# First chunk of the memory tokens loaded from ScalarE's queue, the last square in three pieces, and the low parts of a branch taken one step earlier

## The chip, the cores and the metric

The kernel runs on one core of one Trainium2 chip. The metric is the device time of one execution in microseconds; the kernel before takes 2140.35 us (median of 3 runs, 2139.76 to 2140.51).

## What is computed

One inference step of one encoder layer for two groups of tokens, 256 of a prompt and 64 of a sample, 320 in all, with width 2048:

```python
mkv = rmsnorm(mem_prompt, g_mem[l]) @ w_mem_kv[l]            # 256 memory tokens -> keys and values
xn = rmsnorm(x, g_mix)
(mq, mk, mv, mo, mi, mf, aq, ak, av, iq, ik, iw, cq, gt) = split_in(xn @ w_in)
# branch A: mLSTM; branch B: sparse attention over chosen keys; branch C: attention into the memory tokens
proj = jnp.einsum('btnc,ncd->btnd', branches, w_branch)
merged = jnp.sum(sigmoid(gates) * proj, axis=2)
h = x + merged @ w_out
y = h + (silu(gate) * val) @ w_down                           # [gate|val] = causal conv of rmsnorm(h) @ w_up
y_prompt, y_sample = rmsnorm(y, g_final)
```

All inputs, weights and outputs are float32.

## The kernel before, in words

**Number format.** Every large product is made from three products of float32r numbers: high part times high part, low times high, high times low. A weight arrives as float32 in units of 512 KB (128 rows of 8 blocks of 128 columns). ScalarE casts a unit to its high part (L956), VectorE subtracts to get its low part (L1360), TensorE then uses both (L548 to L550 for most of the kernel, L569 to L591 for the keys and values of the memory tokens). The units go through a ring of four slots: SyncE starts the load of a unit (`load`, L450) when VectorE is done with the slot's last use, and both `split` functions run two units ahead of TensorE (`LEAD`). Results collect in two PSUM banks in turn.

**Order of work.** Each engine has one program, written out by hand, and semaphores tie them together. (1) The memory tokens: 32 units, alternately for keys and values, while the tokens x are normalised. (2) The input projection, with the three branches woven in. (3) The merge: for each of 16 output tiles three gate tiles and three branch products (`merge_tiles`). (4) The output projection. (5) The feed-forward part in four groups, each with 11 pairs of up-projection tiles and then 16 tiles of the down-projection, which are added to `hT`. (6) The final norm.

**The start (L459 to L471, L650 to L671, L992 to L1003, L1458 to L1469).** The SyncE queue issues, one after the other, the first weight unit (L460), the gains of the norms (L461), the first four of the sixteen memory blocks in two transfers of two blocks (L463), three more weight units (L454) and the next four memory blocks (L432). Until the first product can be made TensorE multiplies zeros, `WARM` times (L652); VectorE writes these zeros (L1458) behind six semaphore increments. ScalarE loads a table for Sqrt (L993), casts half of the first unit (L997), waits for the gains and the first two memory blocks, scales these (L971), casts the other half and so on. VectorE makes the low part of the half unit (L1464), then the low parts of the memory blocks (L1388), in step with ScalarE.

**The merge (L1791 in VectorE's program).** In its first tile the last head pair of branch B is still being finished: ScalarE copies its high part out of PSUM (L1199, L1200), VectorE makes the low part (`q_los(3)`, L1764 and L1765). It does so in step m = 1 behind `split(pl, 9 * n + 6 + m)`, the low part of a weight unit. TensorE waits for it ahead of the product of branch B (L860), which is step m = 2.

**The end (L916 to L939, L1300 to L1341, L1942 to L1960).** The down-projection's last tile is added to `hT` by VectorE (L1832), ScalarE squares it (L1259, 320 columns at once) and scales it by the gain (L1303, L1304). The sum of squares over features is a product with a column of ones (`mm`, L598): three with the running sum `hacc`, three with the last square `h2`, each a pass over one group of tokens. Ahead of them TensorE turns the first output batch (`y_turns(0, 1)`, L928). VectorE and ScalarE then work out the inverse root (`rms`, L1374 to L1383), VectorE copies 64 of its values to other partitions for the sample (L1953), and both scale the ten turned batches, even ones on ScalarE (L1339), odd ones on VectorE (L1959). Five stores of 512 KB follow, each behind two batches (`y_store`, L410), four from SyncE's queue and one from ScalarE's.

Of the kernel before, what the change touches and what calls it, by code (L numbers as in the profile page):

```python
# [19 lines left out]
F32 = mybir.dt.float32  # L20
F32R = mybir.dt.float32r
ACT = mybir.ActivationFunctionType
# [65 lines left out]
MEM_SUM, MEM_ROW, X_SUM, X_ROW = 12, 14, 19, 21  # L88
WARM = 22
C_SLOTS = {2: (("scores", 0),), 3: (("probs", 0),), 4: (("values", 0), ("scores", 1)), 5: (("probs", 1),),  # L90
# [98 lines left out]
def layer(nc, a, o):  # L189

    with ExitStack() as ctx:
# [141 lines left out]
        hT = at("hT", R_BC, [KT, T])  # L333
        h2 = at("h_square", R_K + C_COS128 * 4, [T])
        hacc = at("h_square_sum", R_K + (C_COS128 + T) * 4, [3 * P])

# [21 lines left out]
        def sem(name):  # L358
            return ctx.enter_context(nc.semaphore(name))
# [4 lines left out]
        mem_in, x_in = [sem(f"mem_in{n}") for n in range(4)], [sem(f"x_in{n}") for n in range(4)]  # L364
        mem_first, hi_first, lo_first = (sem(n + "_first") for n in ("mem", "w_hi", "w_lo"))
        raw_in = [sem(f"raw_in{n}") for n in range(RING)]
# [33 lines left out]
            sem("f_" + n) for n in ("state", "ext", "tap2", "conv", "tanh", "y", "hi", "lo", "rms"))  # L400
        h_sq, h_sum, h_hi, h_lo, h_g = (sem("h_" + n) for n in ("square", "square_sum", "hi", "lo", "scaled"))
        y_T, y_act, y_dve, y_out, u_out = (
# [27 lines left out]
        def _(sp):  # L430
# [29 lines left out]
            sp.dma_start(raw[:, pl.slot(0), :, :].rearrange("p k c -> p (k c)"), a["w_mem"][0]).then_inc(raw_in[pl.slot(0)], 16)  # L460
            sp.dma_start(gcols[:, :, :].rearrange("p g k -> p (g k)"), a["gain_cols"]).then_inc(gains_in, 16)  # L461
            for n, done in enumerate((mem_first, mem_in[0])):
                sp.dma_start(memT[:, 2 * n:2 * n + 2, :].rearrange("p k t -> p (k t)"),  # L463
                             a["memT"][:, n * 2 * NMEM:(n + 1) * 2 * NMEM]).then_inc(done, 16)
            after = {3: (lambda: mem_chunk(1),), 5: (lambda: mem_chunk(2), identity), 7: (lambda: mem_chunk(3),),
# [63 lines left out]
        def _(pe):  # L529
# [388 lines left out]
            def y_turns(n0, n1):  # L918
                for n in range(n0, n1):
# [9 lines left out]
                    last.then_inc(y_T, 1)  # L929
            y_turns(0, 1)  # L930
            ones = K[:, C_ONE:C_ONE + 1]
            pe.wait_ge(h_sum, 2 * KT + 1)
            for u in range(3):
                mm(M[5][:, u:u + 1], hacc[:, u * P:u * P + P], ones, u == 0, False)
            pe.wait_ge(h_sq, 2 * KT)
            for u in (2, 0, 1):
                last = mm(M[5][0:X_ROWS[u], u:u + 1], h2[:, u * P:u * P + X_ROWS[u]], ones, False, u == 1)
            last.then_inc(sums, 1)
            y_turns(1, len(Y_BATCHES))  # L939

# [3 lines left out]
        @block.scalar  # L944
        def _(act):
            act.sem_inc(f_us, 1)
            act.sem_inc(bank_read[0], 1)
# [48 lines left out]
            for n in range(2):  # L996
                act.copy(whi[:, pl.slot(0), 4 * n:4 * n + 4, :], raw[:, pl.slot(0), 4 * n:4 * n + 4, :])\  # L997
                   .then_inc(w_hi if n else hi_first, 1)
                if n == 0:
                    act.wait_ge(gains_in, 16)  # L1000
                act.wait_ge(mem_in[0] if n else mem_first, 16)
                mem_his(n)
# [253 lines left out]
            def square(pl, e, k, summed):  # L1256
                act.wait_ge(bank_read[pl.bank(e)], pl.bank_read(e))
                act.wait_ge(h_sum, summed)
                act.activation(h2[:, :], hT[:, k, :], ACT.Square).then_inc(h_sq, 1)  # L1259
            for k0, k1, done in ((0, 2, hT_in), (2, KT, hT_rest)):  # L1260
# [38 lines left out]

            def h_tail(pl, e, k):  # L1300

                square(pl, e, k, k + (KT + 2))
                act.activation(hg[:, k, :], hT[:, k, 0:TP], ACT.Identity, scale=gcols[:, 3, ds(k, 1)])  # L1303
                act.activation(hgs[:, k, :], hT[:, k, TP:T], ACT.Identity, scale=gcols[:, 3, ds(k, 1)]).then_inc(h_g, 1)  # L1304
# [23 lines left out]
            for e in range(2):  # L1328
                h_tail(pl, e, KT - 2 + e)

# [16 lines left out]
        def _(dve):  # L1347
            own = Steps(dve, dve_own)
            dve.sem_inc(w_lo, RING)
            dve.sem_inc(c_lo, 2)  # L1350
# [106 lines left out]

            dve.memset(f32(zeros[:, :, :]), 0.0).then_inc(t_zero, 1)  # L1458
            dve.memset(warm[:, :], 1.0).then_inc(t_ones, 1)
# [331 lines left out]
            def merge_tiles(i, stages):  # L1791
                pl = place(U_G, T_G, i, 36, 24)
                for n in range(4):
# [5 lines left out]
                    for m, b in enumerate(BRANCHES):  # L1799
                        t = 6 * n + 3 + m  # L1800
                        split(pl, 9 * n + 6 + m)
                        if n == 0 and m == 1 and stages:
                            q_los(3)
                        dve.wait_ge(w_used, pl.through(9 * n + 6 + m))
                        if m == 0:
                            dve.wait_ge(m_lo, i * 4 + (n + 1))

                        bank = pl.bank(t)
                        dve.scalar_tensor_tensor(gtmp[:, :] if m else acc[:, :], th[:, b, :], 1.0, G[bank][:, 0:T],
                                                 ALU.add, ALU.mult).then_inc(bank_read[bank], 1)  # L1810
                        dve.wait_ge(bank_read[bank], pl.bank_read(t))
                        if m:
                            add = dve.tensor_tensor(acc[:, :], acc[:, :], gtmp[:, :], ALU.add)
                            if m == 1:
                                own.did(add)
                                own.settle()
                            else:
                                add.then_inc(m_sum, 1)
# [15 lines left out]
            def add_square(squared, summed):  # L1834
                dve.wait_ge(h_sq, squared)
                dve.wait_ge(h_sum, summed)
                dve.tensor_tensor(hacc[:, 0:T], hacc[:, 0:T], h2[:, :], ALU.add).then_inc(h_sum, 1)

# [70 lines left out]
            for g in range(GROUPS):  # L1909
# [5 lines left out]
                if g < GROUPS - 1:  # L1915
# [5 lines left out]
                    with dve.Fori(1, KT // 2) as i:  # L1921
                        pl = place(u0, t0, i, 4, 2)
                        for e in range(2):
                            split(pl, 2 * e, 2 * e + 1)
                            add_h(pl, e, i * 2 + e)
            dve.wait_ge(variances, 3)
            dve.memset(hacc[:, :], 0.0).then_inc(h_sum, 1)
            pl = place(u0, t0)
# [15 lines left out]
            add_square(2 * KT - 2, 2 * KT - 1)  # L1944
            for e in range(2):
                add_h(pl, e, KT - 2 + e)
                if e == 0:
                    add_square(2 * KT - 1, 2 * KT)
            dve.wait_ge(sums, 2)
            rms(3, 3, M[5][:, 0:3], fnv)  # L1950
            dve.wait_ge(dve_own, own.n)
            dve.sem_inc(f_rms, 2)
            dve.tensor_copy(fnv[TS:P, 2, 2:3], fnv[0:TS, 2, 2:3]).then_inc(f_rms, 1)  # L1953
            for n in range(1, len(Y_BATCHES), 2):
                u, q = Y_BATCHES[n]
                dve.wait_ge(y_T, n + 1)
                if u == 2:
                    dve.wait_ge(f_rms, 3)
                dve.tensor_scalar(ytok[:, u, q * 4 * P:(q + 1) * 4 * P], y_banks[n % 7][:, :],  # L1959
                                  fnv[:, 2, u:u + 1], None, ALU.mult).then_inc(y_dve, 1)  # L1960


# [235 lines left out]
```

## Time and profile before

| | |
|---|---|
| median of three runs | 2140.35 us (2139.76 to 2140.51) |
| profiled execution, its own time | 2139.86 us |
| its span, first to last instruction | 2138.0 us |
| TensorE busy (matmuls) | 2128.4 us, 100% of the span |
| VectorE / ScalarE / GpSimd busy | 1222.2 / 904.8 / 105.1 us |
| DMA | 329.40 MB, mean 154 GB/s |
| granted TensorE clock | 0.999 |

The span is 1.86 us shorter than the execution's own time; that part lies outside the instructions. Busy times of different engines overlap, so they don't add up to the span. A timeline row gives the start and the duration of an instruction (or of a run of equal ones) in us, the engine, the line, what is written and read, and in brackets how long the engine had been idle and what ended that.

### The profile page before, as it was taken

The numbers are of one execution on the slowest core, as the hardware profiler recorded it, in microseconds if no ns is written. First come the engines' busy times: TensorE is split into PE (matmuls) and PEld (weight loads), VectorE is DVE, ScalarE is ACT, GpSimd is POOL, SyncE is SP. The second block draws the span as 40 slices with busy tenths as digits, with TensorE's granted clock in tenths as the row PEclk, the third lists the DMA queues.
The fourth block names the chain that finished last, engine by engine and source line by source line (L and its number), as shares of the span: only waits on it lengthen the run. The fifth ranks groups of instructions, "written<-read, shape, count | busy, mean of one in ns | idle before, by whom it ended". The sixth has DMA issues, their size and how long they took to land.

```text
span 2138.0 us, 39690 instructions
## 1 busy us (share of the span) xinstructions
PE 2128.4 (100%) x14445; PEld 2107.6 (99%) x14445; DVE 1222.2 (57%) x1933; ACT 904.8 (42%) x1519; POOL 105.1 (5%) x160
## 2 busy tenths in 40 slices
PE   9999999999999999999999999999999999999998
PEld 8899999999999999999999999999999999999998
DVE  7846645545644444443445666656665666656675
ACT  6534433334433333333333444434444444444455
POOL 2203301103200000000000000000000000000000
PEclk9999999999999999999999999999999999999999
DMA  8644444443344444444454444454444444454443
GB/s 314 225 163 134 159 147 149 143 153 124 108 149 148 153 143 151 155 142 154 148 197 156 139 157 142 141 163 143 155 135 158 153 146 139 149 164 148 146 139 130
DMA packets 96607, 329.40 MB, mean 154 GB/s; under 512 B 11640, under 2 KB 19960, under 8 KB 96384
## 3 DMA queue, kind: packets, MB, share of 16 engines
q1 hardware_dynamic: 92624, 315.44, 44.6%
q0 software_dynamic: 3456, 9.49, 1.5%
q10 hardware_dynamic: 432, 3.15, 0.4%
q8 instruction: 67, 1.10, 0.2%
q14 instruction: 28, 0.23, 0.0%
HBM read 321.30 MB, written 6.73 MB: 153 GB/s over the span
## 4 chain that ended last, share of the span: by engine, by line
PE 99%; DVE 0%; DMA 0%; ACT 0%; issue 0%; SPq 0%; DVEq 0%; ACTq 0%
PE bank L550 30%; PE bank L549 30%; PE bank L548 30%; PE bank L598 3%; PE bank L569 1%; PE bank L595 1%; PE bank L586 1%; PE bank L587 1%; PE bank L591 1%; PE bank L906 1%; PE bank L907 1%; PE bank L905 1%; PE bank L571 1%; DMA memT<-in_memT 0%; PE bank L574 0%; PE bank L576 0%
## 5 line engine op out<-in xcount | busy, mean ns | idle before, releaser
L548 PE MATMUL bank<-xn_hi,w_hi 128*128 128x320 f32 (+1 forms) x3088 | 957.5, 310 | 0.0
L550 PE MATMUL bank<-xn_hi,w_lo 128*128 128x320 f32 (+1 forms) x3088 | 952.5, 308 | 0.0
L549 PE MATMUL bank<-xn_lo,w_hi 128*128 128x320 f32 (+1 forms) x3088 | 952.4, 308 | 0.0
L1360 DVE TENSOR_TENSOR w_lo<-w_raw,w_hi 128x1024 fp32r<-128x1024 f32 x625 | 744.8, 1228 | 329.2 <-ACT w_hi L956 327.5
L956 ACT CAST w_hi<-w_raw 128x1024 fp32r<-128x1024 f32 x625 | 631.2, 1047 | 184.8 <-PE bank L550 148.1
L548 PEld LDWEIGHTS bank<-xn_hi,w_hi 128*128 128x128 f32 x3088 | 580.0, 188 | 2.5 <-issue 1.9
L549 PEld LDWEIGHTS bank<-xn_lo,w_hi 128*128 128x128 f32 x3088 | 580.1, 188 | 0.5
L550 PEld LDWEIGHTS bank<-xn_hi,w_lo 128*128 128x128 f32 x3088 | 579.9, 188 | 0.0
L550 PE MATMUL bank<-y_hi,w_lo 128*128 128x320 f32 x616 | 189.9, 308 | 0.0
L548 PE MATMUL bank<-y_hi,w_hi 128*128 128x320 f32 x616 | 189.9, 308 | 0.0
L549 PE MATMUL bank<-y_lo,w_hi 128*128 128x320 f32 x616 | 189.9, 308 | 0.0
L1276 ACT ACTIVATE conv<-u_ext,conv_cols 128x322 f32<-128x322 f32 x88 | 58.0, 659 | 249.5 <-DVE u_ext L1869 249.5
L548 PE MATMUL bank<-branch_hi,w_hi 128*128 128x320 f32 x384 | 118.9, 310 | 0.4 <-DVE branch_lo L1765 0.4
L549 PE MATMUL bank<-branch_lo,w_hi 128*128 128x320 f32 x384 | 118.7, 309 | 0.0
L550 PE MATMUL bank<-branch_hi,w_lo 128*128 128x320 f32 x384 | 118.7, 309 | 0.0
L548 PEld LDWEIGHTS bank<-y_hi,w_hi 128*128 128x128 f32 x616 | 115.6, 188 | 0.0
L549 PEld LDWEIGHTS bank<-y_lo,w_hi 128*128 128x128 f32 x616 | 115.6, 188 | 0.0
L550 PEld LDWEIGHTS bank<-y_hi,w_lo 128*128 128x128 f32 x616 | 115.6, 188 | 0.0
L1832 DVE TENSOR_TENSOR hT<-hT,bank 128x320 f32 (+1 forms) x80 | 39.0, 487 | 131.6 <-PE bank L550 131.5
L963 ACT ACTIVATE gate_tanh<-bank 128x320 f32<-128x320 f32 x48 | 21.0, 438 | 201.8 <-PE bank L550 201.8
L1873 DVE SCALAR_TENSOR_TENSOR conv<-u_ext,conv_cols,conv 128x322 f32<-128x322 f32 x88 | 48.8, 555 | 91.3 <-ACT conv L1276 91.3
L1868 DVE TENSOR_TENSOR u_ext<-bank,ffn_norm_var 128x256 f32<-128x256 f32 x88 | 37.4, 425 | 84.7 <-PE bank L550 83.2
(339 smaller groups left out, 1963.6 us busy)
## 6 DMA issues: line engine op xcount, KB each, us to landing
w_raw<-in_w_in SPq DMA_DIRECT2D x210, 512.0 KB, 3.5
w_raw<-in_w_up SPq DMA_DIRECT2D x176, 512.0 KB, 3.9
w_raw<-in_w_down SPq DMA_DIRECT2D x64, 512.0 KB, 3.5
w_raw<-in_w_branch SPq DMA_DIRECT2D x48, 512.0 KB, 3.3
w_raw<-in_w_mem SPq DMA_DIRECT2D x32, 512.0 KB, 5.3
w_raw<-in_w_out SPq DMA_DIRECT2D x32, 512.0 KB, 4.0
w_raw<-in_w_down SPq DMA_DIRECT2D x64, 192.0 KB, 3.1
xT<-in_xT SPq DMA_DIRECT2D x4, 640.0 KB, 8.7
```

The lines of the kernel that those rows point to most:

```text
L548: pe.matmul(out, h, hi[:, k0 + k, c0:n], start=un == 0 and k == 0, stop=False)
L549: pe.matmul(out, h, lo[:, k0 + k, c0:n], start=False, stop=False)
L550: last = pe.matmul(out, l, hi[:, k0 + k, c0:n], start=False, stop=un == len(units) - 1 and k == nk - 1)
L569: pe.matmul(out[:, :].rearrange("p (s m) -> p s m", s=2), h[:, k, c], mboth[:, :, k_, :], start=k_ == 0, stop=False)
L571: last = pe.matmul(out[:, 0:NMEM], l[:, k, c], mhi[:, k_, :], start=False, stop=k_ == KT - 1)
L598: return pe.matmul(out, lhsT, rhs, start=first, stop=last)
L956: act.copy(whi[:, pl.slot(j), :, :], raw[:, pl.slot(j), :, :]).then_inc(w_hi, 1)
L1276: act.activation(cbuf[:, e, 0:T + 2], ext[:, e, 2:E2], ACT.Identity, scale=ccols[:, 2, ds(col, 1)], bias=ccols[:, 3, ds(col, 1)]).then_inc ...
L1360: dve.tensor_tensor(wlo[:, pl.slot(j), :, :], raw[:, pl.slot(j), :, :], f32(whi[:, pl.slot(j), :, :]), ALU.subtract).then_inc(w_lo, 1)
L1832: dve.tensor_tensor(hT[:, k, :], hT[:, k, :], G[b][:, 0:T], ALU.add).then_inc(bank_read[b], 1)
L1868: dve.tensor_tensor(ext[:, e, 2:2 + TP], G[b][:, 0:TP], fnv[:, 2, 0:TP], ALU.mult)
L1873: own.did(dve.scalar_tensor_tensor(c, ext[:, e, 1:T + 3], ccols[:, 1, ds(col, 1)], c, ALU.mult, ALU.add))
```

## The change

The first four memory blocks are loaded by one transfer of 512 KB from ScalarE's queue, as ScalarE's first instruction, and the gains by a second behind it; both leave SyncE's queue, and the semaphore `mem_first` goes. TensorE's multiplications of zeros become 24, and VectorE writes the zeros ahead of its semaphore increments. In the merge `q_los(3)` is placed ahead of the split of m = 1. The last tile is added and squared in three pieces (128, 128 and 64 columns), and TensorE takes each piece as it comes; `h2` grows from 320 to 384 columns, the last 64 of which are set to zero long before. The first output batch is turned behind the sums. The copy of the 64 values comes behind VectorE's first output batch.

```diff
-WARM = 22
+WARM = 24
...
-        h2 = at("h_square", R_K + C_COS128 * 4, [T])
-        hacc = at("h_square_sum", R_K + (C_COS128 + T) * 4, [3 * P])
+        h2_all = at("h_square", R_K + C_COS128 * 4, [3 * P])
+        h2 = h2_all[:, 0:T]
+        hacc = at("h_square_sum", R_K + (C_COS128 + 3 * P) * 4, [3 * P])
...
# SyncE
             sp.dma_start(raw[:, pl.slot(0), :, :].rearrange("p k c -> p (k c)"), a["w_mem"][0]).then_inc(raw_in[pl.slot(0)], 16)
-            sp.dma_start(gcols[:, :, :].rearrange("p g k -> p (g k)"), a["gain_cols"]).then_inc(gains_in, 16)
-            for n, done in enumerate((mem_first, mem_in[0])):
-                sp.dma_start(memT[:, 2 * n:2 * n + 2, :].rearrange("p k t -> p (k t)"),
-                             a["memT"][:, n * 2 * NMEM:(n + 1) * 2 * NMEM]).then_inc(done, 16)
...
# TensorE
-            y_turns(0, 1)
             ones = K[:, C_ONE:C_ONE + 1]
             pe.wait_ge(h_sum, 2 * KT + 1)
             for u in range(3):
                 mm(M[5][:, u:u + 1], hacc[:, u * P:u * P + P], ones, u == 0, False)
-            pe.wait_ge(h_sq, 2 * KT)
-            for u in (2, 0, 1):
-                last = mm(M[5][0:X_ROWS[u], u:u + 1], h2[:, u * P:u * P + X_ROWS[u]], ones, False, u == 1)
+            for u in range(3):
+                pe.wait_ge(h_sq, 2 * KT + u)
+                last = mm(M[5][:, u:u + 1], h2_all[:, u * P:u * P + P], ones, False, u == 2)
             last.then_inc(sums, 1)
-            y_turns(1, len(Y_BATCHES))
+            y_turns(0, len(Y_BATCHES))
...
# ScalarE
+            act.dma_start(memT[:, 0:4, :].rearrange("p k t -> p (k t)"), a["memT"][:, 0:4 * NMEM]).then_inc(mem_in[0], 16)
+            act.dma_start(gcols[:, :, :].rearrange("p g k -> p (g k)"), a["gain_cols"]).then_inc(gains_in, 16)
...
                 if n == 0:
                     act.wait_ge(gains_in, 16)
-                act.wait_ge(mem_in[0] if n else mem_first, 16)
+                    act.wait_ge(mem_in[0], 16)
                 mem_his(n)
...
+            def last_square():
+                act.wait_ge(h_sum, 2 * KT + 1)
+                for u in range(3):
+                    act.wait_ge(h_last, u + 1)
+                    t = slice(u * P, u * P + X_ROWS[u])
+                    act.activation(h2[:, t], hT[:, KT - 1, t], ACT.Square).then_inc(h_sq, 1)
...
# VectorE
             own = Steps(dve, dve_own)
+            dve.memset(zeros[:, :, :].bitcast(F32), 0.0).then_inc(t_zero, 1)
             dve.sem_inc(w_lo, RING)
...
-                        split(pl, 9 * n + 6 + m)
                         if n == 0 and m == 1 and stages:
                             q_los(3)
+                        split(pl, 9 * n + 6 + m)
...
+            dve.memset(h2_all[:, T:3 * P], 0.0)
             dve.memset(hacc[:, :], 0.0).then_inc(h_sum, 1)
...
-            for e in range(2):
-                add_h(pl, e, KT - 2 + e)
-                if e == 0:
-                    add_square(2 * KT - 1, 2 * KT)
+            add_h(pl, 0, KT - 2)
+            add_square(2 * KT - 1, 2 * KT)
+            dve.wait_ge(w_used, pl.through(3))
+            b = pl.bank(1)
+            for u in range(3):
+                t = slice(u * P, u * P + X_ROWS[u])
+                dve.tensor_tensor(hT[:, KT - 1, t], hT[:, KT - 1, t], G[b][:, t], ALU.add).then_inc(h_last, 1)
+            dve.wait_ge(h_last, 3)
+            dve.sem_inc(bank_read[b], 1)
...
             dve.sem_inc(f_rms, 2)
-            dve.tensor_copy(fnv[TS:P, 2, 2:3], fnv[0:TS, 2, 2:3]).then_inc(f_rms, 1)
             for n in range(1, len(Y_BATCHES), 2):
...
+                if n == 1:
+                    dve.tensor_copy(fnv[TS:P, 2, 2:3], fnv[0:TS, 2, 2:3]).then_inc(f_rms, 1)
```

## Rows read from the trace of the kernel before

**Rows 1.** The page, part 1: busy us of each engine, share of the span.
```profile
PE 2128.4 (100%) x14445; PEld 2107.6 (99%) x14445; DVE 1222.2 (57%) x1933; ACT 904.8 (42%) x1519; POOL 105.1 (5%) x160
```

**Rows 2.** All waits of TensorE's matmuls: waiter, releaser, us in total, times, longest.
```profile
PE bank L652 <- DVE zeros L1458: 2.1, 1, 2.1
PE bank L548 <- DVE branch_lo L1765: 0.4, 1, 0.4
PE bank L569 <- DVE mem_hi_lo L1388: 0.3, 1, 0.3
```

**Rows 3.** Timeline of the first 9 us: start, duration, engine, line, operation.
```profile
0.99 0.40 SPq L460 DMA_DIRECT2D w_raw<-in_w_mem  x1
1.21 1.28 ACT L993 ACT_TABLE_LOAD   x1 [1.21 <-PEq L2188]
...
1.70 0.38 DVE L1458 MEMSET zeros<- 128x384 f32 x1 [1.70 <-PEq L2188]
1.92 0.90 SPq L463 DMA_DIRECT2D memT<-in_memT  x2
...
2.13 5.06 PE L652 MATMUL bank<-zeros 128*128 128x256 f32 x22 [2.13 <-DVE zeros L1458]
...
4.34 0.62 ACT L997 CAST w_hi<-w_raw 128x512 fp32r<-128x512 f32 x1 [1.64 <-DMA w_raw<-in_w_mem]
4.99 0.69 DVE L1464 TENSOR_TENSOR w_lo<-w_raw,w_hi 128x512 fp32r<-128x512 f32 x1 [2.90 <-ACT w_hi L997]
6.20 0.91 ACT L971 ACTIVATE mem_hi_lo<-memT,norm_gains 128x256 fp32r<-128x256 f32 x2 [1.24 <-DMA memT<-in_memT]
...
7.46 0.76 PE L569 MATMUL bank<-mem_hi_lo,w_hi 128*128 128x512 f32 x1 [0.27 <-DVE mem_hi_lo L1388]
...
8.02 0.35 PE L571 MATMUL bank<-mem_hi_lo,w_lo 128*128 128x256 f32 x1
```

**Rows 4.** DMA issues near 2.4 us: count, KB each, median us to landing.
```profile
memT<-in_memT SPq DMA_DIRECT2D x2, 256.0 KB, 4.3
```

**Rows 5.** Timeline of the merge's first tile, ScalarE, VectorE and TensorE.
```profile
600.56 0.27 ACT L1200 CAST branch_hi<-bank 128x128 fp32r<-128x128 f32 x1
...
601.88 1.23 DVE L1360 TENSOR_TENSOR w_lo<-w_raw,w_hi 128x1024 fp32r<-128x1024 f32 x1 [3.29 <-ACT w_hi L956]
603.02 0.68 DVE L1764 TENSOR_TENSOR branch_lo<-bank,branch_hi 128x512 fp32r<-128x512 f32 x1
603.62 0.28 DVE L1765 TENSOR_TENSOR branch_lo<-bank,branch_hi 128x128 fp32r<-128x128 f32 x1
...
603.25 0.31 PE L550 MATMUL bank<-branch_hi,w_lo 128*128 128x320 f32 x1
604.22 0.32 PE L549 MATMUL bank<-branch_lo,w_hi 128*128 128x320 f32 x1
```

**Rows 6.** Timeline of the end, from the last tile's last product on.
```profile
2125.42 0.49 DVE L1832 TENSOR_TENSOR hT<-hT,bank 128x320 f32<-128x320 f32 x1 [3.33 <-PE bank L550]
...
2125.95 0.47 ACT L1259 ACTIVATE h_square<-hT 128x320 f32<-128x320 f32 x1 [3.73 <-DVE hT L1832]
...
2126.47 0.81 PE L598 MATMUL bank<-shape_consts,h_square 128*64 128x1 f32 x6
2126.72 0.33 ACT L1304 ACTIVATE h_scaled_sample<-hT,norm_gains 128x64 f32<-128x64 f32 x1
...
2127.32 0.16 DVE L1374 TENSOR_SCALAR ffn_norm_var<-bank 128x3 f32<-128x3 f32 x1 [1.40 <-PE bank L598]
...
2128.65 0.15 DVE L1953 COPY ffn_norm_var<-ffn_norm_var 64x1 f32<-64x1 f32 x1
2128.83 3.38 DVE L1959 TENSOR_SCALAR y_tokens<-bank,ffn_norm_var 128x512 f32<-128x512 f32 x5
...
2129.66 1.00 SPq L416 DMA_DIRECT2D out_y_prompt<-y_tokens  x2
```

**Rows 7.** DMA between 2129 and 2138 us, in 40 slices: GB/s.
```profile
GB/s 0 0 0 0 0 0 164 400 419 382 382 419 419 419 382 364 437 400 346 437 419 437 400 346 419 419 401 419 382 419 401 400 437 364 437 182 0 0 0 0
```

More of the change, by code:

```diff
@@ L364, in layer @@
         mem_in, x_in = [sem(f"mem_in{n}") for n in range(4)], [sem(f"x_in{n}") for n in range(4)]
-        mem_first, hi_first, lo_first = (sem(n + "_first") for n in ("mem", "w_hi", "w_lo"))
+        hi_first, lo_first = (sem(n + "_first") for n in ("w_hi", "w_lo"))
         raw_in = [sem(f"raw_in{n}") for n in range(RING)]
@@ L400, in layer @@
             sem("f_" + n) for n in ("state", "ext", "tap2", "conv", "tanh", "y", "hi", "lo", "rms"))
-        h_sq, h_sum, h_hi, h_lo, h_g = (sem("h_" + n) for n in ("square", "square_sum", "hi", "lo", "scaled"))
+        h_sq, h_sum, h_hi, h_lo, h_g, h_last = (sem("h_" + n) for n in ("square", "square_sum", "hi", "lo", "scaled", "last_tile"))
         y_T, y_act, y_dve, y_out, u_out = (
@@ L1258, in square @@
                 act.wait_ge(h_sum, summed)
-                act.activation(h2[:, :], hT[:, k, :], ACT.Square).then_inc(h_sq, 1)
+                act.activation(h2, hT[:, k, :], ACT.Square).then_inc(h_sq, 1)
+            def last_square():
[4 more added lines that the diff above has]
+                    act.activation(h2[:, t], hT[:, KT - 1, t], ACT.Square).then_inc(h_sq, 1)
             for k0, k1, done in ((0, 2, hT_in), (2, KT, hT_rest)):
@@ L1298, in up, with h_tail @@
                 conv_inputs(pl, 1, pair, pair + FT)
-            def h_tail(pl, e, k):
-                square(pl, e, k, k + (KT + 2))
+            def h_tail(pl, e, k, last=False):
+                if last:
+                    last_square()
+                else:
+                    square(pl, e, k, k + (KT + 2))
                 act.activation(hg[:, k, :], hT[:, k, 0:TP], ACT.Identity, scale=gcols[:, 3, ds(k, 1)])
@@ L1328, in _ @@
             for e in range(2):
-                h_tail(pl, e, KT - 2 + e)
+                h_tail(pl, e, KT - 2 + e, e == 1)
             root(4, 3, fnv)
@@ L1456, in x_lo @@
                 lo_part(xlo[:, 2 * q:2 * q + 2, :], xsc[:, q % 2, :, :], xhi[:, 2 * q:2 * q + 2, :], n_lo)
-            dve.memset(f32(zeros[:, :, :]), 0.0).then_inc(t_zero, 1)
             dve.memset(warm[:, :], 1.0).then_inc(t_ones, 1)
@@ L1836, in add_square @@
                 dve.wait_ge(h_sum, summed)
-                dve.tensor_tensor(hacc[:, 0:T], hacc[:, 0:T], h2[:, :], ALU.add).then_inc(h_sum, 1)
+                dve.tensor_tensor(hacc[:, 0:T], hacc[:, 0:T], h2, ALU.add).then_inc(h_sum, 1)
             dve.memset(hacc[:, :], 0.0).then_inc(h_sum, 1)
```

## The prediction, made before the changed kernel was run

> **What bounds the kernel now.** First I read the page's busy times: TensorE's matmuls fill 2128.4 of 2138.0 us, VectorE and ScalarE about half of it [rows 1]. So a gain can only come from where TensorE has nothing to do, or from outside its work. Next, the waits of TensorE's matmuls: there are three in the whole execution, 2.1 us for the zeros at the start, 0.3 us for the first memory block, 0.4 us for branch B's low part [rows 2]. That leaves the two ends, which I read in the timeline: from 0 to 7.46 us, before the first real product starts [rows 3], and from 2125.4 us, where the last product of the down-projection is through, to 2138 [rows 6]. In between there is nothing to win but the 0.4 us. The three places of the change are these three, and together they hold some 20 us, most of it transfers and short chains that stay. The change is therefore worth one or two us of 2140, whichever way it goes.
>
> **The merge.** VectorE does the low part of a weight unit at 601.88 (1.23 us) and only then branch B's low part, 603.02 to 603.90. But the high part that it needs was out of ScalarE at 600.56 + 0.27 = 600.83, and VectorE was idle for 3.29 us before 601.88, waiting for the unit's high part [rows 5]. In the new order it takes branch B's part from 600.85 to 601.75 (0.68 and 0.28 us, which overlap a little), and the unit's split still starts at 601.88. So the two operations are hidden by idle time, with 0.1 us to spare; if that cover went, the split would come later by as much, and the product of m = 1, which ran without a wait, does not need that unit (the splits run two units ahead). TensorE started its last product of m = 1 at 603.25 and the second product of branch B at 604.22. At the mean spacing of 2128.4 / 14445 = 0.147 us [rows 1] it would have been 603.54. Gain 0.68 us; the bounds are 0.4, the wait itself [rows 2], and 0.7.
>
> **The end, the last square.** Before: add 2125.42 to 2125.91, square 2125.95 to 2126.42, six passes with the last square 2126.47 to 2127.28, VectorE's first step of the root at 2127.32 [rows 6]. After, the adds of 128, 128 and 64 columns start one behind the other. A piece of 128 columns from PSUM took VectorE 0.28 us [rows 5], and operations in a row overlap by some 0.08, so the adds end near 2125.70, 2125.90 and 2126.05. ScalarE's squares follow each by 0.04; 64 columns take it 0.33 us [rows 6], so the last ends at about 2126.42, as before: the split saves nothing on these two engines. It saves on TensorE, where four of the six passes are over by then. Two are left, a third of 0.81, with their drain about 0.35 us instead of 0.81. Gain 0.46. Bounds: if three adds cost 0.49 each and the square 0.47, the last square ends at 2127.40 and the step is late by 0.47; if the pieces cost no more than the whole (adds 0.49 in all, last square 0.33), it is early by 0.60. I take 0.45.
>
> **The end, the order of turning and copying.** The first output batch is now turned behind the sums. A batch is four fp32 transposes, at 0.135 us a pass (0.81 for six) some 0.5 us, so the two batches that ScalarE and VectorE need first are there 1.1 us after the sums, while the chain of the root takes from 2127.32 to 2128.65, 1.33 us [rows 6]. That hides it; if transposes take 0.1 us more each than I read, the start of the outputs is late by the excess. The copy of the 64 values moves behind VectorE's first batch: that starts at 2128.65 in place of 2128.83, gain 0.18 (bounds 0, if ScalarE's half of the store decides, and 0.18).
>
> What is this worth at the end of the kernel? The stores are the last thing. From 2130.4 to 2137.0 the transfers run at about 400 GB/s without a hole [rows 7]: five stores of 0.52 MB need 6.6 us. VectorE makes a batch in 3.38 / 5 = 0.68 us [rows 6], and so a store is ready every 0.68 us, against 1.3 us that the engines take for it. The end is thus bound by the transfers, and it moves with the first store, not with the last batch. The first store was issued at 2129.66, behind VectorE's first batch; it comes earlier by 0.45 + 0.18 = 0.63 us, and so does the end. Bounds -0.5 and 0.78.
>
> **The start.** Two paths lead to the first product. From the memory blocks: the first two, with their wait counted by ScalarE, were there at about 6.12, ScalarE went on at 6.20, the product started at 7.46, 1.34 us after landing. From the first weight unit: landed at about 4.3, cast 4.34, low part 4.99 to 5.68 [rows 3]. In the new kernel VectorE needs from that landing 0.04 + 0.62 + 0.03 + 0.69 and then the memory block's low part, 0.5 with its hand-over: 1.9 to 1.95 us. Today this path has slack; it won't have any.
> SyncE's queue loses three issues (gains and two of the memory), so weight units 1 to 3 go out about 1.5 us earlier. ScalarE gains two issues ahead of its table load, some 0.45 us each by SyncE's rows, so that the load moves from 1.21 to about 2.1 and ends at 3.4, still ahead of 4.3: hidden. The memory chunk goes out at 1.0 in place of 1.92, but it is 0.52 MB in one piece, and it moves beside the weight unit, not behind it. The rows show no two queues at once at the start, so the price is bounded. Best: both land before TensorE is through with the zeros. The zeros are written first, at about 1.15 instead of 1.70, and TensorE starts at 1.55; 24 products at 5.06 / 22 = 0.23 us take it to 7.05 [rows 3]. Gain at most 0.45. Worst: both land only when the same bytes had landed before, with the second memory transfer at about 2.4 + 4.3 = 6.7 [rows 4]; then the first product is at 6.7 + 1.95 = 8.65, a loss of 1.2. Between them: the weight unit alone had landed at 4.3, and another 0.52 MB at the 400 GB/s of rows 7 add 1.3: both at 5.6, the small gains transfer just behind, the product at 5.6 + 1.95 = 7.55. That is where it was.
> To this comes the clock. The warm-up products have a spacing of 0.23 us for 256 columns, the lower level (1.2 GHz), and the first real one 0.56 us for 512 columns, from 7.46 to 8.02; the next ones run at the upper level. It rose 5.9 us after TensorE began. If it rises as long after the earlier start, at 7.45, the first product loses half of its 0.56. I take +0.2 for the clock and -0.1 for the landing: gain 0.1 us, range -1.2 to +0.75. Behind the first product nothing waits: TensorE has no other wait in the first 26 us [rows 2], and all loads come earlier.
>
> The Trainium skill bears on this: "DMA: Bandwidth & Descriptors", section "Issuing engines are not separate DMA queues", says that transfers started by different engines end up on the same 16 DMA engines and interleave, and that starting them from several engines saves only the issue time. It speaks against this part: by it the memory's lead of 0.9 us is paid for by the first weight unit. No row here shows two queues side by side at the start. Taken at its word, it makes the start worth between nothing and a loss, which is the first rival.
>
> **The sum.** 0.1 + 0.68 + 0.63 = 1.4 us. Profiled execution 2139.86 - 1.4 = 2138.45; the 1.86 us outside the span stay. The median shown, 2140.35, stands 0.49 above the profiled one, so the prediction is 2138.9 us. The other edits (64 columns set to zero by VectorE before the last group's down-projection, three more semaphore steps, a changed address) lie under TensorE's work.
>
> **Rivals.**
> (a) The shared transfer engines: both land at 6.7, the start loses 1.2 and the rest gains 1.31. About 2140.2. For it: the slow landing of rows 4. Against: those were transfers with half-size rows behind the gains.
> (b) The start gains all it can, 0.45 and 0.3 of clock, in all 2.06: 2138.3. For it: the smaller count of issues; against: the weight path's 1.95 us.
> (c) The pieces cost more than they save, -0.47 + 0.18 + 0.68 + 0.1: 0.5 in all, 2139.85. Against: the 0.28 us of rows 5.
> (d) Slower than before: the table load comes first on ScalarE and holds its queue. It ends at 1.21 + 1.28 = 2.49; the memory then needs 4.3 [rows 4] and 0.6 for its other half, the first product is at 7.4 + 1.34 = 8.75. TensorE is idle 1.7 us behind its zeros. The idle time of 0.27 us before did not bring the clock down; if this does, 5.9 us of real work run at the lower level and lose half of that. -1.3 - 2.9 + 1.31 = -2.9: 2143.2. It decides from a first product at about 8.8 without any loss of clock, and earlier with one. For it: the load stands at 1.21, as early as anything on ScalarE. Against: the two issues stand ahead of it in the program.
>
> **Chances.** Forecast (a sum of 0.9 to 1.9 us) 0.60, (a) 0.17, (b) 0.13, (c) 0.04, (d) 0.06. The shown runs lie within 0.75 us, so 0.4 us come on either side. The range 2137.8 to 2140.6 holds the forecast, (b), (c) and most of (a). A measurement can tell a difference of 0.2%, 4.3 us, from no change; none of the cases is that large, (d) included, so "the same" has 0.95, faster 0.02, slower 0.03 for what I have not seen.
>
> **What would show it.** In the changed kernel's waits branch B's low part is gone and its split still starts at about 601.9 less the start's shift. At the end, VectorE's first step of the root comes 1.5 us (before: 1.9) after the first add, and the first store 3.6 us after it (before: 4.24), with a gapless 6.6 us of transfer behind. At the start the first real product is at 7.5; at 7.1 (b) is right, at 8.5 or later (a) or (d), told apart by where the table load stands. The forecast is wrong if a new wait of TensorE appears in the first 30 us, or if the last store no longer ends with the transfers.

## The result and the profile after

The changed kernel takes 2142.43 us (median of 22 runs, 2140.91 to 2143.79); the kernel before, run as often beside it, 2139.86 (2139.13 to 2140.51). The ratio is 1.0013, 95% interval 1.0007 to 1.0019: slower by 2.6 us, where 1.4 us faster was forecast. That is under the 0.2% that the prediction thought could be told from no change, but with 22 runs of each the interval is narrower than that; it is outside the range, and it has a form: 3 of the 22 executions took 2140.9 to 2141.0 us, 13 took 2142.3 to 2142.6, 6 took 2143.4 to 2143.8. The profiled one is of the lowest group (2140.93, span 2139.0), so its trace shows a loss of 1.0 us and not what the median lost on top. In the measurements below, five single executions, of the kernel before too, took 3230 to 9571 us; the ratios leave such slow ones out, and no median shown would move by more than 0.05 us without them.

The waits of TensorE's matmuls in the changed kernel, which answer to [rows 2]:

```profile
PE bank L566 <- DVE mem_hi_lo L1397: 2.2, 1, 2.2
PE bank L649 <- DVE zeros L1357: 1.6, 1, 1.6
PE bank L595 <- ACT h_square L1264: 0.2, 1, 0.2
```

Branch B's wait is gone and the zeros come 0.5 us earlier, but the wait ahead of the first real product has grown from 0.3 to 2.2 us. The timeline of the start, to be read beside [rows 3]:

```profile
0.99 0.42 ACTq L942 DMA_DIRECT2D memT<-in_memT  x1
0.99 0.40 SPq L461 DMA_DIRECT2D w_raw<-in_w_mem  x1
...
1.43 0.46 ACTq L943 DMA_DIRECT2D norm_gains<-in_gain_cols  x1
...
1.58 5.49 PE L649 MATMUL bank<-zeros 128*128 128x256 f32 x24 [1.58 <-DVE zeros L1357]
...
2.13 1.28 ACT L991 ACT_TABLE_LOAD   x1 [2.13 <-issue]
...
6.29 0.62 ACT L995 CAST w_hi<-w_raw 128x512 fp32r<-128x512 f32 x1 [2.66 <-DMA w_raw<-in_w_mem]
...
7.99 0.91 ACT L969 ACTIVATE mem_hi_lo<-memT,norm_gains 128x256 fp32r<-128x256 f32 x2 [1.08 <-DMA norm_gains<-in_gain_cols]
...
9.25 0.47 PE L566 MATMUL bank<-mem_hi_lo,w_hi 128*128 128x512 f32 x1 [2.19 <-DVE mem_hi_lo L1397]
```

And from issue to landing, the DMA issues of 0.9 to 1.2 us and the gains of 1.4 us:

```profile
memT<-in_memT ACTq DMA_DIRECT2D x1, 512.0 KB, 5.4
w_raw<-in_w_mem SPq DMA_DIRECT2D x1, 512.0 KB, 5.3
norm_gains<-in_gain_cols ACTq DMA_DIRECT2D x1, 32.0 KB, 6.5
```

The first weight unit lands at 6.3 us instead of 4.3. The memory chunk is there at 6.4, where its two halves had landed at about 6.1 and 6.7. But ScalarE goes on only at 7.99, and the releaser is not the memory: it is the 32 KB of gains, 6.5 us on their way. The first real product starts at 9.25 instead of 7.46.

The end, beside [rows 6]:

```profile
2126.22 0.61 DVE L1960 TENSOR_TENSOR hT<-hT,bank 128x128 f32<-128x128 f32 x3 [3.32 <-PE bank L547]
2126.61 0.66 ACT L1264 ACTIVATE h_square<-hT 128x128 f32<-128x128 f32 x3 [3.59 <-DVE hT L1960]
2126.97 0.83 PE L595 MATMUL bank<-shape_consts,h_square 128*128 128x1 f32 x6 [0.22 <-ACT h_square L1264]
...
2127.84 0.16 DVE L1383 TENSOR_SCALAR ffn_norm_var<-bank 128x3 f32<-128x3 f32 x1 [1.00 <-PE bank L595]
...
2130.02 1.31 SPq L417 DMA_DIRECT2D out_y_prompt<-y_tokens  x2
```

From the last tile's first add to the root's first step it takes 1.62 us (1.90 before), to the first store 3.80 (4.24), and to the end of the span 12.78 (12.58 before): the end does not follow the first store. So the profiled execution adds up: first product 1.79 us later, of which some 0.3 come back because it now runs at the upper clock level (0.43 us from its start to that of the third product instead of 0.75), merge -0.68, end +0.20: 1.0, the difference of the spans.

### The profile page after: what moved, and what is told of

It is laid out like the page before. It is cut to its first block, busy times and chain, and to the rows that moved or that the text cites. A ratio compares the mean times of both kernels' runs of the same rounds, so it can differ in the third digit from the quotient of the medians.

```text
span 2139.0 us, 39699 instructions
## 1 busy us (share of the span) xinstructions
PE 2128.2 (99%) x14447; PEld 2107.8 (99%) x14447; DVE 1223.7 (57%) x1936; ACT 905.2 (42%) x1521; POOL 105.8 (5%) x160
## 4 chain that ended last, share of the span: by engine, by line
PE 99%; DMA 0%; DVE 0%; ACT 0%; issue 0%; ACTq 0%; DVEq 0%
PE bank L545 30%; PE bank L547 30%; PE bank L546 30%; PE bank L595 3%; PE bank L566 1%; PE bank L592 1%; PE bank L583 1%; PE bank L584 1%; PE bank L588 1%; PE bank L904 1%; PE bank L903 1%; PE bank L902 1%; PE bank L568 1%; DMA norm_gains<-in_gain_cols 0%; PE bank L925 0%; PE bank L571 0%
```

## The experiments

In each, the times are medians of the run beside the kernel before on the same chip. Most ratios have an interval of ±0.1%, 2 us, that touches 1: by the ratio alone only e3 is clear of no change, and the rest lean on the profiles and on how the single executions lie. A single median of 11 moves by 0.2 to 0.3 us, so for the end I read the profile, from the last tile's first add to the end of the span. Five kernels with the old end show 12.49 to 12.59 us there (the kernel before, e1, e3, e7, e8).

**e1_merge_only.** The edit is the merge's alone:

```diff
-                        split(pl, 9 * n + 6 + m)
                         if n == 0 and m == 1 and stages:
                             q_los(3)
+                        split(pl, 9 * n + 6 + m)
```

> The kernel before with only the low part of branch B ahead of the weight split. Theory: TensorE's wait of 0.4 us goes and nothing takes its place, 0.7 us less than the kernel before, in every execution. Rival: the split comes later by the two operations and TensorE waits for it one unit on, no difference (within 0.1 us).

2139.23 us against 2139.70 (ratio 0.9998, 0.9989 to 1.0007): 0.5 us of the 0.7 expected, in a median that can be off by 0.2. The wait is gone from the profile, and the low part stands where the idle time was:

```profile
601.09 0.69 DVE L1764 TENSOR_TENSOR branch_lo<-bank,branch_hi 128x512 fp32r<-128x512 f32 x1 [2.35 <-ACT branch_hi L1200]
601.70 0.28 DVE L1765 TENSOR_TENSOR branch_lo<-bank,branch_hi 128x128 fp32r<-128x128 f32 x1
601.97 1.23 DVE L1360 TENSOR_TENSOR w_lo<-w_raw,w_hi 128x1024 fp32r<-128x1024 f32 x1
```

**e2_tail_only.** The changes at the end alone, start and merge as before (WARM = 22).

> The kernel before with only the changes at the end (last square in three pieces, first batch turned behind the sums, copy behind VectorE's first batch). Theory: from the last product on it is shorter by 0.2 to 0.5 us, so 0.2 to 0.5 us less than the kernel before, with no more spread than before. Rival: the whole loss of the changed kernel sits here, since its profile shows 12.83 us from the last product to the end of the span against 12.63: 0.2 us or more longer than before.

2140.01 against 2139.70 (1.0001, 0.9992 to 1.001), the end at 12.76: it loses 0.2 us instead of gaining, as the rival had it, but that is a twelfth of the loss and not all of it.

**e3_start_only.** The changes at the start alone.

> The kernel before with only the changes at the start (memory chunk and gains from ScalarE's queue, zeros first, 24 multiplications of zeros). Theory: the first real product starts at 9.2 to 9.3 us in place of 7.46, so the shortest executions are 1.5 us longer than the kernel before; most of the others are longer by another 1.5 or 2.6 us, because TensorE is idle for 2.2 us and part of the executions show a granted clock of 0.998: median 2142.8 to 2143.3. Rival: the start costs nothing by itself because TensorE catches up on what was bound by transfers: within 0.3 us of the kernel before, and the spread is not from here.

2142.95 against 2139.70 (1.0015, 1.0006 to 1.0024), and three groups again: two executions at 2141.3 and 2141.4, five at 2142.8 to 2143.0, four at 2144.0 to 2144.2. The whole loss is here. The profiled execution was of the highest group and shows how it differs. TensorE's stretches (length, matmuls' busy time with their number in brackets, granted clock as a share of 2.4 GHz, DMA share, GB/s):

```profile
5.00:6.00 1.00, 1.00 (x10) 1.00 1.00 370
6.00:7.00 1.00, 0.22 (x2) 1.00 1.04 405
7.00:8.00 1.00, 0.00 (x0) 1.00 1.04 417
8.00:9.00 1.00, 0.00 (x0) 0.72 1.01 414
9.00:10.00 1.00, 0.81 (x3) 0.50 1.04 426
14.00:15.00 1.00, 1.00 (x5) 0.50 0.92 315
15.00:16.00 1.00, 1.00 (x6) 0.87 1.00 348
```

TensorE was through with the zeros at 6.2 and idle for 2.97 us; in that idle time its clock fell to the lower level (0.50 of 2.4 GHz) and came back only after 15 us. Nearly 6 us of real products, from 9.19 on, ran at half speed: about 2.9 us, the distance from the lowest group to the highest (2.8). The idle time was longer than the 2.19 us of the changed kernel's profile because the 24 zeros took 4.64 us and not 5.49: their pace rose from about 5 us on (10 products between 5 and 6 us, where the changed kernel had 6). The clock's column shows 1.00 in both, so while the zeros run the level has to be read from the products' spacing.

**e4_warm32.** `WARM = 32` in the changed kernel, nothing else.

> The changed kernel with 32 instead of 24 multiplications of zeros, which end at about 8.9 us and leave TensorE idle for 0.3 us ahead of its first real product, as in the kernel before. Theory (idle time brings the clock down for a stretch): all executions fall on the lowest of the changed kernel's levels, 2140.9 to 2141.0, with a clock of 1.0. Rival (the levels come from the transfers or from the clock's phase whatever TensorE does): three levels as before, median 2142.4.

All 11 executions at 2140.84 to 2141.05, on the lowest group: the spread is made by the clock and goes with more zeros. What I expected of the mechanism was not right: the zeros did not end at 8.9. In the profile 32 products took 5.39 us, less than the 24 of the changed kernel (5.49), because the clock rose among them: between 5 and 6 us it did 11 products, where the changed kernel did 6:

```profile
5.00:6.00 1.00, 1.00 (x6) 1.00 0.98 342
```

TensorE was idle for 2.21 us all the same, and the times show a fall in none of the 11. Two readings fit, and no run parts them: more work ahead of the gap holds the clock up, or the eight zeros more keep the gap from growing to the 2.97 us of e3 where the clock rises early.

**e5_gains_sync.** The gains back on SyncE's queue, behind the first weight unit:

```diff
+            sp.dma_start(gcols[:, :, :].rearrange("p g k -> p (g k)"), a["gain_cols"]).then_inc(gains_in, 16)
...
-            act.dma_start(gcols[:, :, :].rearrange("p g k -> p (g k)"), a["gain_cols"]).then_inc(gains_in, 16)
```

> The changed kernel with only the 32 KB of gains moved back to SyncE's queue, behind the first weight unit; the memory chunk stays on ScalarE's queue. Theory (the gains come late because they stand behind 512 KB on ScalarE's queue): they land by 6.4 us instead of 7.9, the first product is bound by the weight unit (landing at 6.3, then 1.95 us) and starts at 8.2 to 8.3 us in place of 9.25; TensorE is idle for 1.2 us at most and the lower levels of the clock go: 2139.9 to 2140.1 in nearly all executions. Rival (the transfer engines are simply full, whatever the order): the first product within 0.3 us of 9.25 and the same three levels.

2139.89 against 2139.84 (1.0001, 0.9992 to 1.001); 8 of 11 at 2139.8 to 2139.9, three at 2141.3 to 2141.4. The first product starts at 8.18, as expected:

```profile
6.29 0.62 ACT L995 CAST w_hi<-w_raw 128x512 fp32r<-128x512 f32 x1 [3.15 <-DMA w_raw<-in_w_mem]
6.82 0.91 ACT L969 ACTIVATE mem_hi_lo<-memT,norm_gains 128x256 fp32r<-128x256 f32 x2
...
8.18 0.47 PE L567 MATMUL bank<-mem_hi_lo,w_hi 128*128 128x512 f32 x1 [1.51 <-DVE mem_hi_lo L1397]
```

The place of one transfer of 32 KB is 1.07 us of the start and most of the falls of the clock, 2.5 us of the median. What is left is the weight unit, which still lands at 6.3, so the first product is 0.72 us later than before. The gains were not quick here either. In the second place of SyncE's queue they took 3.0 us in the kernel before, with nothing on ScalarE's queue, and now, beside the memory chunk:

```profile
norm_gains<-in_gain_cols SPq DMA_DIRECT2D x1, 32.0 KB, 5.2
```

They land at 6.65, just early enough not to hold up ScalarE, which casts the weight unit until 6.91.

**e6_units_held.** SyncE waits for the gains ahead of weight units 1 to 3:

```diff
+            sp.wait_ge(gains_in, 16)
```

> The changed kernel with SyncE holding back weight units 1 to 3 until the gains have landed, so that nothing but the first unit, the memory chunk and the gains moves before. Theory (two 512 KB transfers side by side delay each other, the units behind them only add to it): unit and chunk land near 5.6 and the gains near 5.8, the first product at 7.6 to 7.9, but the next units land later. Rival (the units behind are what delays the gains and nothing else): the first unit lands at 4.3 as in the kernel before and the first product starts at 7.1. If neither helps (landing still past 6.2), the slow landing is that of a queue by itself.

2140.76 against 2139.84 (1.0005, 0.9996 to 1.0014), with a first product at 8.03:

```profile
memT<-in_memT ACTq DMA_DIRECT2D x1, 512.0 KB, 5.3
w_raw<-in_w_mem SPq DMA_DIRECT2D x1, 512.0 KB, 5.1
norm_gains<-in_gain_cols ACTq DMA_DIRECT2D x1, 32.0 KB, 5.0
```

The first unit lands at 6.1 (6.3 in the changed kernel). Neither the theory's 5.6 nor the rival's 4.3: two 512 KB transfers side by side, with nothing else under way but the gains, need 5.1 and 5.3 us, where the unit with the others behind it on one queue needed 3.3. From 2 to 6 us they moved at 160, 328, 406 and 188 GB/s, 1.08 MB in all. The gains land 5.0 us after issue instead of 6.5: of their 3.5 us above the kernel before, 1.5 are the three units on the other queue and 2.0 the two large transfers. The median is longer than e5's, although the first product is earlier, in part because the units held back come late: TensorE waits 0.3 us at 11.4.

**e7_warm10.** `WARM = 10` in the kernel before, the transfers untouched.

> The kernel before with 10 instead of 22 multiplications of zeros, which end at about 4.4 us, so that TensorE is idle for 3.1 us and no transfer is changed. Theory (the levels come from the clock, which falls or does not rise when TensorE is idle): the median is longer than the kernel before by 1.5 to 3 us, most executions at 2141.2 or 2142.5 with a granted clock of 0.998 to 0.999. Rival (the levels come from the transfers of the changed start): no difference, 2139.9.

2141.64 against 2139.84 (1.0008, 0.9998 to 1.0017). The idle time in front of the first product, at 7.34, is 2.71 us, and the products run at the lower level's spacing until 11.8 us (the kernel before: until 8.0). So the clock costs about 1.8 us in the median without any change of a transfer, by fewer zeros and the longer idle time behind them; here it had not risen before the gap, so this is no fall. Clean groups as in e3 are not seen.

**e8_merge_zeros.** The merge's order, and the zeros written first with 26 multiplications, on the kernel before.

> The kernel before with the merge's new order and the zeros written first, 26 multiplications; transfers and the end as before. Theory: 0.7 us from the merge, and up to 0.3 us more where the clock rises ahead of the first product; median 2138.9 to 2139.1, less spread than with the merge alone. Rival (the zeros' position is worth nothing): 2139.2, as with the merge alone.

2139.07 against 2139.84 (0.9996, 0.9987 to 1.0005). The median fits, but the profiled execution took 2141.86 (the kernel before beside it had two such, 2141.74 and 2141.86); in it the memory landed late, the first product started at 8.84, TensorE was idle for 2.03 us, and the clock fell in the middle of the first products and rose again at 12.6 (columns as in e3):

```profile
9.00:10.00 1.00, 1.00 (x5) 0.62 1.03 422
10.00:11.00 1.00, 1.00 (x5) 0.50 1.04 426
12.00:13.00 1.00, 1.00 (x6) 0.67 0.91 373
```

Some 3.4 us at half speed are an estimated 1.7 us, near the 1.5 us that the middle group of the changed kernel lost. What the zeros' place gives over e1 (0.77 us gained against 0.47, on two chips) is about what the medians can be off by.

**e9 to e11: the end taken apart.** e9 moves only the copy, e10 is the whole end with `y_turns(0, 1)` ahead of the sums as before, e11 only turns the first batch behind the sums.

> The kernel before with only the copy of the 64 values moved behind VectorE's first output batch. In the kernel before the first store is issued 4.24 us after the first add of the last tile and the last store 6.87 us after it. Theory (the end hangs on the last store, which comes behind the last batch): first store at 4.06, last store unchanged at 6.9, the end of the span unchanged within 0.1 us, median 2139.7 to 2139.9. Rival (the end is bound by the transfers from the first store on, as the prediction had it): the end 0.18 us earlier.

> All of the changes at the end except that TensorE turns the first output batch ahead of the sums, as in the kernel before. Theory (TensorE's row of passes and turns sets the last batch; with all batches turned behind the sums it idles for 0.2 us first): the root's first step is 0.2 us later than with the whole of the change, but the last store comes 0.3 us earlier, near 6.6 us after the first add, and the end 0.2 to 0.3 us earlier than in the kernel before. Rival (transfer-bound): the end follows the first store, later than with the whole of the change.

> The kernel before with only the first output batch turned behind the sums. Theory: TensorE waits 0.5 us for the last square with nothing to do and its last turn is 0.5 us later, so the last store and the end of the span are later by 0.4 to 0.5 us. Rival (transfer-bound): the first store is unchanged and so is the end, within 0.1 us.

The profiles, in us from the first add: e9 has its first store at 4.07, its last at 7.00 and its end at 12.32; e10 at 3.85, 6.78 and 12.81; e11 at 4.24, 7.15 and 12.59. The medians, 2139.41, 2139.91 and 2139.92 against 2139.89, don't speak against it. e9 and e11 refute the theory: the end follows the first store (0.26 us earlier in e9, where the first store is 0.17 earlier and the last one later) and doesn't care for the last (e11). That is what the prediction had said. But e10 has its first store 0.39 us earlier and a later end. So there is something else in the kernels with pieces, and the transfers of the last microseconds show it, here e2 between 2131 and 2132 us (queue, packets, MB, share):

```profile
q1 hardware_dynamic: 112, 0.39, 99.9%
q14 instruction: 1, 0.01, 1.9%
```

One packet of an instruction queue, 1.9% of 16 engines for 1 us, which is 0.3 us of one engine. It stands in each of the profiles so far with the pieces (the changed kernel, e2, e4, e5, e6, e10), 6.2 to 6.4 us after the first add, and in none without them (the kernel before, e1, e3, e7, e8, e9, e11), where no such packet falls between the first add and the end of the span. The bulk of the stores is through earlier, but a few engines seem to trail: by an estimate of 400 / 16 = 25 GB/s for each, the 73, 18 and 36 GB/s in the last slices of e2 are one to three engines (GB/s, 2129 to 2138 in 40 slices):

```profile
GB/s 0 0 0 0 273 437 400 364 400 400 455 401 382 364 400 419 346 437 419 400 437 328 419 437 364 473 382 383 437 364 437 401 400 73 18 36 0 0 0 0
```

**e12_combined.** Run together with e9 to e11. The start's transfers as before, zeros first (26), merge, and e10's end.

> The changed kernel with the transfers of the start as before (all on SyncE's queue), zeros first with 26 multiplications, the merge's new order, and the end with the first batch turned ahead of the sums. Theory: the merge's 0.7 us and 0.2 to 0.3 us at the end, median 2138.7 to 2138.9, below both kernels. Rival: the end gives nothing, 2139.1, as with merge and zeros alone.

2139.32 against 2139.89 (0.9998, 0.9989 to 1.0007), the end at 12.83, with the packet among the stores here too: the rival.

**e13_pad_vector and e14_pad_scalar.** e2 with instructions added that do nothing, so that the fetch falls elsewhere; e14 has them on ScalarE:

```diff
+            for _ in range(16):
+                dve.sem_inc(unused, 1)
             pl = place(UNITS - 4, T_END - 2)
```

> All of the changes at the end, with 16 increments of an unused semaphore on VectorE ahead of the last pair of tiles, in time that VectorE has free. Theory (a packet of the instruction queue lands among the stores and holds one transfer engine back): if VectorE's instructions are what it fetches, the packet moves to before 2129 us, the trickle behind the stores goes, and the span ends 12.1 to 12.2 us after the last tile's first add in place of 12.79. If the packet stays (it is another engine's) the end stays. Rival (the late end comes from the pieces themselves): the packet moves and the end stays at 12.8.

> The same with the 16 increments on ScalarE in place of VectorE. Theory: if the packet is ScalarE's it moves to before 2129 us and the span ends 12.1 to 12.2 us after the first add. Rival: the packet moves and the end stays at 12.8.

On VectorE the packet leaves the stores and the end comes 12.05 us after the first add; on ScalarE the packet stays and so does the end, 12.76. The stores' issues are the same in both (3.79, 5.40, 6.07, 6.86). In e13, between 2131 and 2132 us, and its slices from 2129 to 2138:

```profile
q1 hardware_dynamic: 118, 0.42, 102.6%
```

```profile
GB/s 0 0 0 0 0 309 437 382 419 382 419 419 382 455 328 419 401 401 455 382 400 419 346 419 419 382 455 364 419 419 346 473 346 419 37 0 0 0 0 0
```

The slices end without a trail. The packet now stands ten us earlier, between 2121 and 2122:

```profile
q14 instruction: 1, 0.01, 2.5%
```

The medians agree: 2139.31 (0.9997, 0.9987 to 1.0007) and 2140.06 (1.0001, 0.9991 to 1.0011) against 2139.57, of 8 executions each. So 0.7 us of the end hang on where an instruction fetch falls. How 0.3 us of one engine's time come to 0.7 us of the end stays open.

**e15_no_pieces and e16_all_but_queues.** e15: merge, zeros first, and the copy, on the kernel before. e16: the changed kernel with the start's transfers as before, 26 multiplications, and the 16 increments.

> The kernel before with the merge's new order, the zeros first (26), and the copy behind VectorE's first batch; transfers of the start and the last square as before. Theory: 0.7 us from the merge and 0.2 us from the copy (the end 12.32 us after the first add): median 2138.8 to 2139.0, the fastest of all. Rival: the copy gives nothing, 2139.1.

> The changed kernel with the start's transfers back on SyncE's queue, 26 multiplications of zeros, and 16 increments of an unused semaphore on VectorE ahead of the last pair of tiles. Theory: the merge's 0.7 us and the end's 0.5 us add up, median 2138.3 to 2138.6, the fastest kernel of all, with the span's end 12.0 to 12.1 us after the last tile's first add. Rival (the parts interfere): 2138.9, as with merge and copy alone.

e15 takes 2138.87 against 2139.57 (0.9995, 0.9986 to 1.0004), 0.7 us less where 0.9 was expected, its end at 12.39. e16 takes 2138.35 against 2139.80 (0.9993, 0.9983 to 1.0002), its end at 12.10: 1.45 us less than the kernel before, the parts add up, and it is the fastest of all. The interval of the ratio still touches 1, but its executions (8891.39 left out) lie at 2138.02 to 2138.93, below every one of the kernel before (2139.38 and up).

## Why the prediction was wrong

**The merge** was right in place and mechanism: 0.68 us expected, the wait gone, its split not late for anybody; 0.5 us in the median, 0.68 in the profile's account.

**The end** was right in its chain up to the first store and wrong in what follows. The last square in pieces: I had taken 0.45, measured 0.28. The term that was off is "Two are left" (of the six passes): the first piece's square is through only 0.29 us earlier than the whole one was (0.71 against 1.00 us after the first add), and behind it TensorE's six passes took 0.83 us in a row, as many as before (0.81), so TensorE and not the last piece sets the sum. The copy gave 0.15 to 0.18 of its 0.18 us. The first batch turned behind the sums cost the first store nothing, as forecast (3.80 in e2, 3.85 in e10). So the first store came 0.44 us earlier, not 0.63. That the end follows it was right (e9, e11, and e13 with 0.5 us gained). What failed is that the end "moves with the first store" in every case: VectorE's longer program brought an instruction fetch into the stores. I had looked at no instruction queue.

**The start** is the step that failed: "both at 5.6, the small gains transfer just behind". The rate was too high, since I took the 400 GB/s of the stores for the first transfers of the program: the other 0.52 MB added 2.0 us to the landing of the weight unit and not 1.3, so that unit and chunk landed at 6.3 and 6.4, and e6 shows 1.8 us (6.1) with nothing but the gains beside them. The rival (a) had priced this nearly right, with 6.7. "Just behind" was the dearer error: ScalarE and VectorE wait for the gains before anything else, and 32 KB behind 512 KB, beside a busy second queue, took 6.5 us in place of 3.0; they landed 1.5 us behind the chunk. Of the 1.79 us the gains' place is 1.07 and the weight unit 0.72 (e5). The rule of the Trainium skill in "DMA: Bandwidth & Descriptors", section "Issuing engines are not separate DMA queues", that starting transfers from several engines saves only the issue time, is borne out by these runs: the memory's 0.9 us of earlier issue brought the whole chunk no earlier (6.4, between the 6.1 and 6.7 of its halves) and cost the weight unit 2.0 us. I had weighed it and put it at 0.17.

**The clock.** I had it falling only in the rival (d), for another cause (the table load, which stood at 2.13 behind both issues, hidden as forecast), and elsewhere as a gain of 0.2, for which I had read the rise as coming 5.9 us after TensorE began; in e3 the zeros ran faster after some 3.5 us. The gap that I had at nothing was 2.2 us in a profile without a fall and 2.97 us in the one with a fall from before the first product. (d)'s price, half of 5.9 us and 2143.2 in all, is nearly what the highest group and e3 show; that is luck for the number, since nothing of (d)'s cause happened. Of the median's loss of 2.6 us about 1.5 is this (2142.4 against 2140.9), and e4 takes it away.

**The number.** The forecast of 2138.9 added 0.49 us because the median of three runs stood above the profiled one; with 22 runs the kernel before is at 2139.86, where the profiled one was. Without it the same terms give 2138.45.

What stays open: why the clock fell with 2.03 us of idle time in one execution of e8 and with 2.2 us in none of e4 (one of whose 11 was profiled), and what distinguishes the middle group, of which no execution was profiled. Which engine's fetch each instruction queue carries was seen only for q14 and VectorE.

## What to carry to other kernels

Ahead of the first product, count what every engine waits for first, and put the smallest of these transfers behind the first operand rather than behind the second (e5): its place cost more here, 1.07 us, than the megabyte around it, 0.72. The very first place was not tried. A gap in TensorE's work is priced twice, by its length and by the products that run at the lower clock behind it, and the second part comes and goes from run to run, so one profile may not show it. When an end bound by stores doesn't follow its first store, look for an instruction fetch among the stores before doubting the chain.

## What the runs showed of the hardware

- Two transfers of 512 KB started together from two queues at the beginning of a program landed after 5.3 and 5.4 us (5.1 and 5.3 with only 32 KB beside them, e6); the first one with the others behind it on one queue landed after 3.3.
- A transfer of 32 KB landed after 3.0 us behind 512 KB on the only queue in use, 5.2 us in the same place beside a second queue's 512 KB (e5), 5.0 us behind the second queue's 512 KB (e6), and 6.5 us there with three more units on the first queue.
- The granted clock fell from its upper level (2.4 GHz) to the lower one (1.2 GHz) in an idle stretch of 2.97 us, and nearly 6 us of products ran at half speed behind it (e3). Behind 2.03 us of idle time it fell once the products had begun, for some 3.4 us (e8); behind 2.19 and 2.21 us it did not fall. 24 multiplications of zeros took 4.64 us in one execution (e3), 5.09 in another (e5) and 5.49 in the changed kernel's: whether the clock rises among them differs from run to run.
- A single instruction packet among 2.6 MB of stores came with an end 0.7 us later (12.76 against 12.05 us) and a trail of 18 to 73 GB/s behind the bulk. 16 instructions more on VectorE moved it ten us earlier, 16 on ScalarE left it where it was.
